# Wide experts of a two-layer mixture network: two buffers of rounded pieces and a ring of eleven pieces

## What is computed

```python
def swiglu(h, w1, w3, w2):
    return (jax.nn.silu(h @ w1) * (h @ w3)) @ w2

def moe_swiglu(h, w_r, w1e, w3e, w2e):
    logits = (h @ w_r).astype(jnp.float32)
    vals, idx = lax.top_k(logits, TOP_K)
    wts = jax.nn.softmax(vals, axis=-1)
    comb = jnp.sum(jax.nn.one_hot(idx, N_EXPERTS, ...) * wts[..., None], axis=-2)
    for e in range(N_EXPERTS):
        out = out + comb[..., e:e + 1] * swiglu(h, w1e[e], w3e[e], w2e[e])
```

## Time and profile before

| | us |
|---|---|
| runs, median of 3 (lowest, highest) | 1992.03 (1986.04, 1992.1) |
| the profiled execution, its own time | 1990.12 |
| its span, first to last instruction | 1988.3 |
| PE busy in the span | 1792.1 (90%) |
| DVE busy | 821.2 (41%) |
| ACT busy | 520.2 (26%) |
| DMA | 476.23 MB, mean 240 GB/s |

### The profile page before, as it was taken

The page is one execution under the profiler, slowest core; times in us unless marked ns, Lnnn a source line. Parts: engine busy times, 40 slices in busy tenths (PEclk is TensorE's granted clock), DMA queues, the critical chain, the costliest instruction groups (busy, mean ns, idle before and its releaser), DMA issues.

```text
span 1988.3 us, 19498 instructions
## 1 busy us (share of the span) xinstructions
PE 1792.1 (90%) x7958; PEld 1118.0 (56%) x7958; DVE 821.2 (41%) x1146; ACT 520.2 (26%) x648; POOL 5.0 (0%) x14
## 2 busy tenths in 40 slices
PE   6999989899999998997989899887887988887886
PEld 3344454488887774386778688523236873332323
DVE  3233442444444663144388788401017860010102
ACT  4221032600000004212367567200005740000001
POOL 0000000000000000000000000000000000000000
PEclk9999999999999998897899999998998999988887
DMA  9322393523222214222469799699999989999994
GB/s 358 114 102 110 111 387 137 169 85 121 91 74 85 81 37 172 85 85 85 170 252 375 264 329 376 242 394 394 394 395 356 374 301 343 396 392 395 393 394 164
DMA packets 223830, 476.23 MB, mean 240 GB/s; under 512 B 9907, under 2 KB 32725, under 8 KB 223701
## 3 DMA queue, kind: packets, MB, share of 16 engines
q1 hardware_dynamic: 222176, 474.24, 65.2%
q10 hardware_dynamic: 1524, 0.21, 0.1%
HBM read 473.38 MB, written 1.05 MB: 239 GB/s over the span
## 4 chain that ended last, share of the span: by engine, by line
PE 75%; SPq 11%; DMA 5%; issue 3%; DVE 3%; ACT 2%; ACTq 0%; DVEq 0%
PE ps L658 9%; SPq L543 8%; PE ps L963 6%; PE ps L664 6%; PE ps L665 6%; PE ps L666 6%; PE ps L1033 6%; PE ps L1035 6%; PE ps L1040 6%; DMA ring<-in_e_w 4%; PE ps L829 4%; SPq L547 3%; PE ps L720 3%; PE ps L704 3%; PE ps L989 2%
## 5 line engine op out<-in xcount | busy, mean ns | idle before, releaser
L963 PE MATMUL ps<-ring,work 128*64 128x512 f32 x1120 | 284.8, 658 | 82.4 <-DMA ring<-in_e_w 64.8
L963 PEld LDWEIGHTS ps<-ring,work 128*64 128x64 f32 x1120 | 91.1, 151 | 252.5 <-issue 252.5
L1982 DVE TENSOR_TENSOR mixT<-work,ps 64x256 f32<-64x256 f32 x70 | 29.7, 424 | 420.6 <-ACT work L1428 419.5
L1542 DVE TENSOR_TENSOR ring_rounded<-ring,hT_rounded 128x2048 fp32r<-128x2048 f32 x84 | 191.6, 2288 | 26.4 <-ACT hT_rounded L1447 19.9
L658 PE MATMUL ps<-hT,ring 128*128 128x512 f32 (+2 forms) x544 | 182.4, 494 | 0.0
L1447 ACT CAST hT_rounded<-ring 128x2048 fp32r<-128x2048 f32 x84 | 159.9, 1910 | 43.8 <-PE ps L1035 34.2
L658 PEld LDWEIGHTS ps<-hT,ring 128*128 128x128 f32 (+1 forms) x544 | 99.6, 185 | 80.2 <-issue 73.0
L664 PE MATMUL ps<-mixT_rounded,work_rounded 128*128 128x512 f32 x352 | 138.3, 393 | 6.0 <-DVE hT_rounded L1542 5.2
L665 PE MATMUL ps<-hT_rounded,work_rounded 128*128 128x512 f32 x352 | 138.1, 392 | 0.0
L666 PE MATMUL ps<-mixT_rounded,ring_rounded 128*128 128x512 f32 x352 | 137.9, 392 | 0.0
L989 PE MATMUL ps<-ring,mixT 128*64 128x512 f32 x560 | 125.8, 593 | 0.0
(11 more groups left out here) (228 smaller groups left out, 2398.7 us busy)
## 6 DMA issues: line engine op xcount, KB each, us to landing
ring<-in_e_w SPq DMA_DIRECT2D x336, 1024.0 KB, 13.9
ring<-in_w_mod SPq DMA_DIRECT2D x24, 2048.0 KB, 14.8
ring<-in_w_in SPq DMA_DIRECT2D x12, 2048.0 KB, 11.8
ring<-in_w SPq DMA_DIRECT2D x22, 1024.0 KB, 7.9
ring<-in_w_out SPq DMA_DIRECT2D x4, 2048.0 KB, 13.2
ring<-in_w SPq DMA_DIRECT2D x4, 2048.0 KB, 7.8
ring<-in_w SPq DMA_DIRECT2D x2, 1536.0 KB, 6.6
mixT<-in_ctx SPq DMA_DIRECT2D x2, 512.0 KB, 4.2
```

The source lines that it names most:

```text
L963: ins = pe.matmul(acc[H * w:H * w + H, :], x[:, k, 0:H], piece_words(e, b, 2 * half + w)[:, kk * BLK:(kk + 1) * BLK], start=(k == 0), stop ...
L1542: return dve.tensor_tensor(dst, src, high, ALU.subtract)
```

## The change

There are two buffers of rounded pieces instead of three, so that the cast of piece n waits for piece n - 2. The words of the third, part of `norms`, become an eleventh place of the ring: the words for the DMA, and the same words seen as rounded for the low part. In the first round the places of the old ring are filled as the last users of the earlier stages' slots finish. The eleventh is filled when the last modulation, which is the last to use those words of `norms` before the experts, is done.

```diff
-ESLOTS = 2 * SLOTS
+ESLOTS = 2 * SLOTS + 1
...
-HIGHS = 3
+HIGHS = 2
...
-        highs = [x_low[:, 0:4, :].rearrange("p a b -> p (a b)"), x_low[:, 4:8, :].rearrange("p a b -> p (a b)"),
-                 norms_r[:, 2:6, :].rearrange("p a b -> p (a b)")]
+        highs = [x_low[:, 0:4, :].rearrange("p a b -> p (a b)"), x_low[:, 4:8, :].rearrange("p a b -> p (a b)")]
+
+        norm_words = {id(ring): norms[:, 2:6, :].rearrange("p a b -> p (a b)"),
+                      id(ring_r): norms_r[:, 2:6, :].rearrange("p a b -> p (a b)")}
...
         def piece_words(e, b, i, of=ring):
             s = piece(e, b, i)[0]
+            if s == ESLOTS - 1:
+                return norm_words[id(of)]
             return of[:, s * PIECE:(s + 1) * PIECE]
...
-                    if turn_ == 0:
+                    if turn_ == 0 and s < 2 * SLOTS:
                         sp.wait_ge(tile_ready, chunk_last[last_chunk[s // 2]] + 1)
+                    elif turn_ == 0:
+                        sp.wait_ge(h_ready, 2 * DEPTH * KD)
                     else:
                         wait_free(sp, e * PER + PLACE[b, i] - ESLOTS)
```

## The result

The changed kernel takes 2011.74 us (median of 4 runs, 2010.74 to 2012.65), the kernel before 1990.0 us over its 4 runs (1986.04 to 1992.1). The ratio is 1.0112, with a 95% interval of 1.0097 to 1.0127: about 22 us slower. The profiled execution took 2011.23 us with a span of 2009.4, 21.1 us more than the span of before. The forecast was +13.5 us, from a median of 1992.03 to 2005.5, with a range of 1992 to 2014. The way and the place were right. The size was 8 us too little: +21.7 us between the medians.

The account below looks back on a forecast made before the run. The prediction took wide experts as bound by PE and narrow ones by the weight stream. Its terms, 13.7 + 5.1 - 5.3 = +13.5 us, took the median from 1992.03 to 2005.5 us; range 1992 to 2014.

Parts of the forecast that it names:

- The eleventh piece: Ring: the two DMA-bound narrow runs each start with 11 MB landed, not 10; 2 x 2.66 = 5.3 us gained.
- The middle costs nothing: Inside wide experts' blocks: casts and low parts waiting on two buffers still arrive in time; cost 0.
- The waits at the end: End of each wide expert: late casts delay ACT and DVE, so (6,4) starts 4.57 us later; three ends, 13.7 us.
- The clock: TensorE drops to its lower clock in the 4.1 us hole before (6,4): 1.70 us each, 5.1 for three.
- the dear bound: Upper bound on slow matmuls after the hole before (6,4): about 2.8 us each, read after expert 1's 7.68 us hole.
- the dear clock: Forecast variant pricing the lower TensorE clock after the holes before (6,4) at its upper bound: +16.8 us in all.
- the eleventh piece that does nothing: Rival: SP issues the ring's added piece too late, so no gain; +18.8 us, 2010.8 us, chance 0.04.
- The end hides it: Rival, wide experts' ends: ACT and DVE are in time, the hole stays 1.40 us; -5.3, 1986.7 us, chance 0.14.
- each narrow expert gains a piece: Rival: the ring gains 13.3 us over five narrow experts; +5.5, 1997.5 us, chance 0.05.
- The clock stays: Rival: TensorE keeps its full clock through the holes at wide experts' ends; +8.4, 2000.4 us, chance 0.22.

## Why the prediction was right, and where its size was off

- **The eleventh piece, -5.3.** Right: -3.08 and -2.26 in experts 2 and 5, nothing in 3 and 6. Removing it cost 5.6; beside a third buffer or a reordered end it gave 3.7 and 3.8. Its first transfer was issued at 987.64 us, 16 us ahead of the experts, and cost nothing there.
- **The middle costs nothing.** Right: 2.72 us a piece, no wait of PE within blocks, and with the reordered end experts 0, 1 and 4 take as long with two buffers as with three.
- **The waits at the end, 3 x 4.57 = 13.7.** Right, step by step: turn at +1.87 forecast, hole 2.28 instead of 0.41 measured; hole before (6,4) 4.1 forecast, 4.11 measured. The two moves show that it is the order on ACT and DVE that makes them. The three ends' holes grew by 3 x 1.88 + 3 x 2.71 = 13.8 us.
- **The clock, 5.1.** This is the term that was mis-sized. The ends grew by 8.81, 9.13 and 6.94 us, 24.9 in all; without the 13.8 of waiting 11.1 are left. Two steps of it failed. First, I priced only the hole before (6,4) and put the one ahead of the turn at nothing, without a word on it. It is shorter than the 3.23 us that had kept the clock, but the clock fell there in experts 0 and 1, for 1.6 us each, and not in expert 4. Second, I took 1.70 us from the narrow experts' holes of 3.44 us; behind (6,4) it was 2.58, 2.92 and 2.34 (from the first matmul of (6,4) to the gather's end), close to the dear bound of 2.5 to 2.8 that I had read from expert 1's beginning.
- **The sum.** 13.8 + 11.1 - 5.3 = 19.6 us, plus 1 us ahead of the experts and 0.5 spread over the rest: 21.1.
- **The range.** That it held the measured time is in part luck. The forecast with the dear clock was +16.8 us, and +21.7 is beyond it. The upper bound of 2014 came from another case, the eleventh piece that does nothing, which did not happen; and the kernel before measured 2 us less over its four runs than the 1992.03 from which I started.
- **The rivals.** "The end hides it" and "each narrow expert gains a piece" fell with the two rows above; the latter becomes true with eight places. "The clock stays" fell: it is lost in five of six holes.

## What to carry to other kernels

Count a buffer's worth at the places where the engine that waits for it (here PE) has no other work between two dependent steps: here the steady state had 0.9 us to spare, and two late casts out of 42, those of (5,5) and (6,5), made the whole loss. When a buffer is taken away, look at what stands in program order behind the operation that it delays; moving two operations ahead of it on ACT and DVE won back more than the buffer had given. A ring's place is worth about one landing for each time the ring gets full ahead of a stretch bound by DMA, so count those times in the DMA share before adding or removing one.

## What the chip showed that I had not expected

- A hole of 2.28 us on TensorE, between dense matmuls, lost the full clock in 10 of 12 cases, while 3.23 us kept it in a narrow expert: in two of three in the changed kernel and with the turned block alone moved, in all three with two buffers and a ring of 10 and of 8. The price was about 1.6 us each. The hole of 4.11 us lost it in all 15 cases of five kernels, at very different prices: 2.3 to 2.9 us in the changed kernel, 1.6 with the first hole filled, 2.9, 1.6 and 1.4 with the gate alone moved. What decides between losing and keeping it, and the price, was not found.
- Matmuls that nobody reads keep the clock (1.00 in the window where it had been 0.50), but the longer code came with new waits of 1.65 and 3.92 us inside the first piece of two experts.
